# Two layers of attention, short convolution and mixture of experts on one core: router work between the projection's products, counting behind the first gather, constant products in TensorE's pauses, gathered rows taken in halves

## The reference

```python
for i in range(DEPTH):
    xn = rms_norm(h, norm_mix[i])
    mix = sliding_window_attention(...) if i % 2 == 0 else gated_short_conv(...)
    h = h + mix
    h = h + hierarchical_moe(rms_norm(h, norm_ffn[i]), ...)
return rms_norm(h, final_norm)

# inside hierarchical_moe, T tokens
g_prob, g_idx = top_k(softmax(xt @ w_group + b_group), 1)
in_group = (xt @ w_expert + b_expert) of the chosen group
e_prob, e_local = top_k(softmax(in_group), 2)
out[t] = sum over its two experts e of gate * ((silu(x @ g_e) * (x @ u_e)) @ w_down[e])
```

## Time and profile before

| what | us |
|---|---|
| median of three runs | 1453.46 |
| the profiled execution's own time | 1453.89 |
| its span | 1452.2 |
| TensorE busy (matmul) | 1280.6 |
| VectorE / ScalarE / GpSimd busy | 405.7 / 336.3 / 133.2 |
| granted TensorE clock, mean | 0.937 |
| HBM read | 444.96 MB |

### The profile page before, as it was taken

The page is one execution under the profiler, slowest core; times in us unless marked ns, Lnnn a source line. Parts: engine busy times, 40 slices in busy tenths (PEclk is TensorE's granted clock), DMA queues, the critical chain, the costliest instruction groups (busy, mean ns, idle before and its releaser), DMA issues.

```text
span 1452.2 us, 15480 instructions
## 1 busy us (share of the span) xinstructions
PE 1280.6 (88%) x6014; PEld 688.8 (47%) x6014; DVE 405.7 (28%) x867; ACT 336.3 (23%) x632; POOL 133.2 (9%) x109
## 2 busy tenths in 40 slices
PE   5968897998999989999489998799999989999991
PEld 4844675443344333433168877654343433443330
DVE  5376232111111111111455454321111211111114
ACT  3249321221112111221231121212111211121112
POOL 5070020010000000000000000201000100000000
PEclk9978997999999999999779999889999999999996
DMA  9200227999999999999722232479999999999974
GB/s 353 72 1 1 116 115 291 436 429 427 432 432 430 428 429 435 429 429 402 270 60 88 87 118 114 200 318 425 428 434 429 431 428 431 433 429 430 427 298 196
DMA packets 55497, 456.01 MB, mean 314 GB/s; under 512 B 13924, under 2 KB 29310, under 8 KB 38308
## 3 DMA queue, kind: packets, MB, share of 16 engines
q1 hardware_dynamic: 44084, 444.29, 73.0%
q0 software_dynamic: 5120, 8.41, 1.5%
q10 hardware_dynamic: 6256, 2.80, 0.8%
HBM read 444.96 MB, written 18.90 MB: 319 GB/s over the span
## 4 chain that ended last, share of the span: by engine, by line
PE 54%; DMA 35%; DVE 6%; ACT 4%; issue 1%; SPq 0%; POOLq 0%; DVEq 0%; ACTq 0%
DMA big<-in_moe_w_gate_up_dram 33%; PE ps L1015 22%; PE ps L834 19%; PE ps L1033 5%; PE ps L993 3%; DVE xr L1154 1%; PE ps L938 1%; ACT arena L659 1%; ACT arena L675 1%; PE ps L820 1%; PE ps L1005 1%; DVE arena L1249 1%; PE ps L914 1%; DVE h L1293 1%; DVE h L1291 1%
## 5 line engine op out<-in xcount | busy, mean ns | idle before, releaser
L1015 PE MATMUL ps<-big,arena 128*64 128x512 f32 x2048 | 470.5, 615 | 49.8 <-DMA big<-in_moe_w_gate_up_dram 47.3
L1015 PEld LDWEIGHTS ps<-big,arena 128*64 128x64 f32 x2048 | 151.3, 142 | 362.7 <-issue 293.6
L1375 DVE TENSOR_TENSOR gain<-arena,ps 64x512 f32<-64x512 f32 x64 | 68.5, 1070 | 458.8 <-ACT arena L721 458.8
L721 ACT ACTIVATE arena<-ps 64x512 f32<-64x512 f32 x64 | 37.7, 589 | 530.5 <-PE ps L1015 530.5
L540 POOL DMA_INDIRECT rows<-arena x64 | 62.4, 975 | 912.5 <-DVE arena L1401 912.5
L1033 PE MATMUL ps<-small,arena 128*64 128x512 f32 x512 | 116.9, 598 | 0.0
L834 PE MATMUL ps<-xt_parts,small_parts 128*128 128x512 f32 x288 | 112.2, 399 | 1.5 <-DVE xr_parts L1163 1.5
L834 PE MATMUL ps<-xr_parts,small_parts 128*128 128x512 f32 x272 | 107.3, 394 | 0.0
L834 PE MATMUL ps<-xt_parts,big_parts 128*128 128x512 f32 x256 | 100.1, 391 | 0.0
L993 PE MATMUL ps<-arena_parts 128*128 128x512 f32 x256 | 85.5, 416 | 0.0
L993 PE MATMUL ps<-xr_parts,arena_parts 128*128 128x512 f32 x256 | 81.4, 400 | 0.0
(11 more groups left out here) (156 smaller groups left out, 1271.0 us busy)
## 6 DMA issues: line engine op xcount, KB each, us to landing
big<-in_moe_w_gate_up_dram SPq DMA_DIRECT2D x62, 4096.0 KB
small<-in_moe_w_down_dram SPq DMA_DIRECT2D x32, 2048.0 KB, 19.3
arena<-in_moe_w_down_dram SPq DMA_DIRECT2D x16, 2048.0 KB, 18.4
xt<-in_moe_w_down_dram SPq DMA_DIRECT2D x16, 2048.0 KB, 17.8
big<-in_conv_w_in_dram SPq DMA_DIRECT2D x12, 1024.0 KB, 9.2
big<-in_moe_w_gate_up_dram SPq DMA_DIRECT2D x8, 1024.0 KB, 17.6
big<-in_attn_w_qkv_dram SPq DMA_DIRECT2D x1, 4096.0 KB
big<-in_attn_w_o_dram SPq DMA_DIRECT2D x1, 4096.0 KB
```

The costliest lines, as they stand in the source:

```text
L721: nc.scalar.activation(silu[BLOCK:P, j, :], ps[2 + j][0:BLOCK, :], ACT.Silu).then_inc(S.silu_ready, 1)
L1015: mm = nc.tensor.matmul(ps[2 + j][half * BLOCK:(half + 1) * BLOCK, :], xg[:, k, j * BLOCK:(j + 1) * BLOCK], w[:, k, half * FF:(half + 1) * ...
L1375: V.tensor_tensor(hid[BLOCK:P, j, :].rearrange("q (k p) -> q p k", p=P), silu[BLOCK:P, j, :].rearrange("q (p k) -> q p k", p=P), ps[2 + j] ...
```

## The change

Five things: `turn_tile(i, t - 1)` moves into the middle of tile t of the projection, and `logits(t - 1)` behind its second half; ScalarE's and VectorE's copies of tile t-1 move ahead of the norm step of tile t to match; the marks move from `rt` into the tile `silu`, so that counting (`count`) can stand behind the first gather; `keep_busy` multiplies the identity with itself into bank 5, where nobody reads the result, three times before turn(3) and five times after logits(3); and the gathered rows and their transposes are handed over in halves of 512 columns, by three counts of `gathered` and four of `rows_taken` in place of two and two.

```diff
--- before.py
+++ after.py
@@ -179,6 +179,7 @@
         where_f = cut(2)
         where = cut(2).bitcast(I32)
         picked = rt.rearrange("p t c -> p (t c)")
+        marks = silu.rearrange("p a b -> p (a b)")[:, 0:TT * E].rearrange("p (t e) -> p t e", e=E)
         hid = gain[:].rearrange("p (j f) -> p j f", j=2)
 
         early = xt[:].rearrange("p (a k b) c -> p a k (b c)", a=2, k=2)
@@ -623,8 +624,10 @@
 
             def norm(i):
                 for t in range(TT):
+                    if t >= 1 and i in (1, 3):
+                        take_turned(i, t - 1)
                     root(i, t)
-                    if t >= 1 and i < 4:
+                    if t >= 1 and i in (0, 2):
                         take_turned(i, t - 1)
                 if i < 4:
                     take_turned(i, TT - 1)
@@ -702,18 +705,18 @@
 
             def take_picked(S, i):
 
-                act.wait_ge(S.gathered, i * 2 + 1)
+                act.wait_ge(S.gathered, i * 3 + 1)
                 for half in range(2):
-                    ins = nc.scalar.activation(picked[:, half * HALF:(half + 1) * HALF], ps[half][:], ACT.Copy)
-                ins.then_inc(S.rows_taken, 1)
+                    nc.scalar.activation(picked[:, half * HALF:(half + 1) * HALF], ps[half][:], ACT.Copy)\
+                        .then_inc(S.rows_taken, 1)
 
             def take(S, i):
 
-                act.wait_ge(S.gathered, i * 2 + 2)
                 for half in range(2):
-                    ins = nc.scalar.activation(xg[:, 4 * half:4 * half + 4, :],
-                                               ps[half][:].rearrange("p (a b) -> p a b", a=4), ACT.Copy)
-                ins.then_inc(S.rows_taken, 1)
+                    act.wait_ge(S.gathered, i * 3 + half + 2)
+                    nc.scalar.activation(xg[:, 4 * half:4 * half + 4, :],
+                                         ps[half][:].rearrange("p (a b) -> p a b", a=4), ACT.Copy)\
+                        .then_inc(S.rows_taken, 1)
 
             def swish(S, n, j):
 
@@ -939,6 +942,12 @@
                                           start=(d == 0), stop=(d == DT - 1))
                 mm.then_inc(logits_ps, 1)
 
+            def keep_busy(n):
+
+                for _ in range(n):
+                    nc.tensor.matmul(ps[5][:], ident[:], ident[:].unsqueeze(1).to_broadcast([P, 4, P]),
+                                     start=True, stop=True)
+
             def project(first, i, product):
 
                 for t in range(TT):
@@ -952,13 +961,14 @@
                                 mm = product(ps[6 + f % 2][:], t, half, k)
                             if k == DT - 1:
                                 mm.then_inc(mix_ps, 1)
+                            if t >= 1 and half == 0:
+                                turn_tile(i, t - 1)
                     if t >= 1:
-                        turn_tile(i, t - 1)
-                    if t >= 2:
-                        logits(i // 2, t - 2)
-                logits(i // 2, TT - 2)
+                        logits(i // 2, t - 1)
+                keep_busy(3)
                 turn_tile(i, TT - 1)
                 logits(i // 2, TT - 1)
+                keep_busy(5)
 
             def attention_product(bank, t, half, k):
                 if t == 0 and half == 0:
@@ -974,14 +984,16 @@
             def router(l):
                 pe.wait_ge(mask_ready, l + 1)
                 ranks = ps[5][:, 0:TT * E].rearrange("p (t e) -> p t e", e=E)
-                nc.tensor.matmul(ranks[:, 0:TT], upper[:], rt[:, :, 224:256], start=True, stop=False)
+                nc.tensor.matmul(ranks[:, 0:TT], upper[:], marks, start=True, stop=False)
                 for t in range(TT - 1):
                     mm = nc.tensor.matmul(ranks[:, t + 1:TT], ones[:],
-                                          rt[:, t:t + 1, 224:256].to_broadcast([P, TT - 1 - t, E]),
+                                          marks[:, t:t + 1, :].to_broadcast([P, TT - 1 - t, E]),
                                           start=False, stop=(t == TT - 2))
                 mm.then_inc(rank_ps, 1)
+
+            def count(l):
                 for t in range(TT):
-                    mm = nc.tensor.matmul(ps[7][:, 0:E], ones[:], rt[:, t, 224:256], start=(t == 0), stop=(t == TT - 1))
+                    mm = nc.tensor.matmul(ps[7][:, 0:E], ones[:], marks[:, t, :], start=(t == 0), stop=(t == TT - 1))
                 mm.then_inc(rank_ps, 1)
 
             def pick(S, i):
@@ -1000,11 +1012,13 @@
                 for t in range(TT):
                     nc.tensor.matmul(ps[4][:, 0:2], parts(sel[:, t].rearrange("p j s -> p (j s)")), parts(dcol[:, t, :]),
                                      start=(t == 0), stop=(t == TT - 1))
-                pe.wait_ge(S.rows_taken, i * 2 + 1)
                 for d in range(DT):
+                    if d % 4 == 0:
+                        pe.wait_ge(S.rows_taken, i * 4 + d // 4 + 1)
                     mm = nc.tensor.transpose(ps[d // 4][:, (d % 4) * P:(d % 4 + 1) * P],
                                              picked[:, d * P:(d + 1) * P], ident[:])
-                mm.then_inc(S.gathered, 1)
+                    if d % 4 == 3:
+                        mm.then_inc(S.gathered, 1)
 
             def gate_up(S, j, w, cuts=None):
 
@@ -1040,12 +1054,13 @@
                 b0 = BIG_EXPERT[l]
                 pe.wait_ge(x_split, TT * (l + 1))
                 pick(S, 0)
+                count(l)
                 turn_picked(S, 0)
 
                 def up(i, j):
                     big_loaded(pe, b0 + j, i)
                     if j == 0:
-                        pe.wait_ge(S.rows_taken, i * 2 + 2)
+                        pe.wait_ge(S.rows_taken, i * 4 + 4)
                     gate_up(S, j, big[:, big_slot(b0 + j)])
 
                 def turn(m, odd, j):
@@ -1087,7 +1102,7 @@
                                 q = r * PAIRS + i - PAIRS
                                 pick(over[l], q)
                                 turn_picked(over[l], q)
-                                pe.wait_ge(over[l].rows_taken, q * 2 + 2)
+                                pe.wait_ge(over[l].rows_taken, q * 4 + 4)
                                 pe.wait_ge(over[l].where_ready, q + 1)
                                 pe.wait_ge(over_in[l], (r * PAIRS + i + (1 - PAIRS)) * 64)
                                 for j in range(2):
@@ -1278,6 +1293,8 @@
 
                     for half in range(2):
                         f = 2 * t + half
+                        if half == 1 and t >= 1:
+                            take_turned(2 * l + 1, t - 1)
                         dve.wait_ge(mix_ps, 2 * TT * l + f + 1)
                         hs = h[:, t, half * HALF:(half + 1) * HALF]
                         V.tensor_tensor(hs, ps[6 + f % 2][:], hs, ALU.add).then_inc(mix_used, 1)
@@ -1309,7 +1326,7 @@
                 idx = rt[:, :, 120:128].bitcast(U32)
                 gs, s2 = rt[:, :, 128:129], rt[:, :, 129:130]
                 m2 = rt[:, :, 192:224]
-                m12 = rt[:, :, 224:256]
+                m12 = marks
                 io = iota[:, 0:E].unsqueeze(1).to_broadcast([P, TT, E])
                 dve.wait_ge(logits_ps, TT * (l + 1))
                 step(V.tensor_tensor(lg, ps[4][:, 0:TT * NR].rearrange("p (t n) -> p t n", t=TT),
@@ -1379,7 +1396,7 @@
 
             def find_rows(S, i, taken=None):
 
-                dve.wait_ge(S.gathered, i * 2 + 2)
+                dve.wait_ge(S.gathered, i * 3 + 3)
                 if taken is not None:
                     dve.wait_ge(S.row_ready[0], taken)
                 for j in range(2):
```

## The result

The changed kernel takes 1444.86 us (median of five, 1443.28 to 1445.16), the kernel before beside it 1453.46 us: ratio 0.9931, interval 0.9911 to 0.995. On a second chip session it took 1442.0 us against 1454.41, ratio 0.9917, 0.9902 to 0.9932. So it is faster, by 0.7% in one session and 0.8% in the other; 1440.0 was forecast. The profiled execution took 1443.71 us, span 1441.8, 10.4 less than before; 14.6 had been the sum and 13.5 the forecast.

A forecast was written before the change was run, and what follows sets the result against it. Experts bound by weight loads, so each layer's end follows its stream's start, limited by TensorE's path and the DMA backlog. Gains of 7.9 and 6.7 us sum to 14.6, less 1.1 is 13.5: 1440.0 us, range 1438 to 1447.

The forecast's parts named there:

- the sum: First gate/up product of both layers: the lesser gains of the two limits add up to 14.6 us.
- the forecast proper: Whole kernel: 1440.0 us, within 1438 to 1443, given a chance of 0.60.
- rival 1: Clock falls in the router's pause, ranks and gather at half clock in both layers: 6.6 us lost, 1446.6; chance 0.20.
- One of its own signs of being wrong: Gather ahead of the experts: the forecast is wrong if it runs at half clock; 3.85 us was expected.
- The last product pushed by 3.1 and 2.6 us: End of projection: turns and logits between products delay the last one, 3.1 us in layer 0, 2.6 in layer 1.
- The stall of turn(0): Middle of tile 1 of layer 0's projection: the turn waits for its row, 0.5 us.
- Turn(3) at 214.5 us: Behind layer 0's projection: the last turn starts with its row, at 214.5 us for 215.64 before.
- Turn to last logits 3.44 us at full clock: From turn(3)'s start to the end of the last logits: 3.44 us at full clock for 6.24 before.
- Constant products cost nothing as long as the clock is full, and it is full: Waits before turn(3) and under VectorE's router: 0.87 us each, three 2.6 and five 4.4 us, fitting inside the waits.
- Counting and halves: Gather to first gate/up product: 3.2 us for 3.5; counting there eats most of the halves' gain of about 1 us.
- Two limits that tie: Start of the gate/up stream: TensorE's path allows 7.9 and 6.8 us gain, the DMA backlog 7.9 and 6.7.
- The end moves with the start: Experts of each layer: DMA-bound at 428 GB/s, so the layer's end moves with its stream's start, some 7 us earlier.

The follow-up runs named there:

- a4: Changed kernel plus two constant products per layer, one behind turn(3) and one between ranks and first gather: 1442.23 us, ratio 0.9915 to before.
- c4: b4 with one more constant product, between ranks and counting: 1436.95 us, ratio 0.9868 to before.
- a3: Changed kernel with counting back in front of the first gather, marks left in their new place: 1441.64 us, ratio 0.9916 to before.
- c2: Changed kernel with gathered rows handed over whole again, one count for both copies and eight transposes in a row: 1441.58 us, ratio 0.9905 to before.
- b2: a3 with each layer's first gather leaving out the remainder of the tokens (8 of its 16 products): 1440.75 us, ratio 0.9893 to before.
- c1: Kernel before plus only the constant products, three ahead of logits(2) and five behind the last logits: 1441.12 us, ratio 0.9902 to before.
- b1: Changed kernel with turns, logits and copies in the old order, three constants between logits(1) and logits(2): 1440.02 us, ratio 0.9894 to before.
- a1: Changed kernel again without any edit, in the second session: 1442.0 us, ratio 0.9917 to before.
- b4: Changed kernel with old order, earlier VectorE copy of tile 2, counting first, constants ahead of logits(2), behind turn(3) and five under the router: 1437.09 us, ratio 0.9863.
- c3: The same kernel as b4, run again for a second sample: 1437.16 us, ratio 0.9863 to before.
- b3: Changed kernel with ten constant products in place of five under the router: 1446.58 us, ratio 0.9937 to before.

## Why the prediction came out as it did

The sign and the range held, and so did the main mechanism, the clock. The size was too large by 3.1 us in the profiled execution (10.4 for 13.5), by 4.9 on the first medians: 1444.86 lies outside the 1438 to 1443 of the forecast proper and is in the range because this takes in rival 1; the 1442.0 of the second session lies inside. One of its own signs of being wrong came true in part: the gather of layer 1 ran at half clock for 3.4 of its 5.47 us.

- **The last product pushed by 3.1 and 2.6 us:** right, 3.35 and 2.9. The stall of turn(0) was 0.5 us, as worked out.
- **Turn(3) at 214.5 us:** 214.79.
- **Turn to last logits 3.44 us at full clock:** 3.9. A turn that is followed by a wait takes 1.11 us on the chain, not 0.87, and logits behind a copy 1.95, not the 1.71 of those that run on.
- **Constant products cost nothing as long as the clock is full, and it is full:** this step failed. The price of one, 0.87 us, was right. But in each layer the clock fell once, for 3.4 us: in layer 0 the five took 6.06 us and stuck out by 0.8 behind the mask, in layer 1 the gather took 5.47 us, 1.6 too many. I had read the full clock of the 3.7 us from 236.7 as proof that light work with short pauses is safe. The windows of after show 3.5 us of just that, from 214.9, and half clock behind them. Rival 1 had named the router's pause at 6.6 us; what came was about a third of it, 0.8 and 1.6 us. With a constant product in either light stretch (a4, c4) the clock stayed at 1.00, and in c4 it cost nothing; but it also stayed there in some layers without, so how far such a constant can be relied on is open.
- **Counting and halves:** gather to gate/up 3.0 us for 3.2; a3 and c2 give 0.4 against and 0.5 for, as forecast that the one eats the other.
- **Two limits that tie:** partly. With the clock's loss TensorE's path was the later one, by pauses of 1.2 and 2.1 us. The backlog as second limit shows at most in b2, for 0.6 us.
- **The end moves with the start:** right to 0.3 us in both layers.
- **What I had not seen** is that the new order is no part of the gain: I credited the whole path to one change, where c1 and b1 show that constants in the old order do as much. Before, turn(3) came as late as 215.64 us because logits(2) ahead of it ran at half clock; in c1 they run at full clock and turn(3) starts at 213.47, earlier than the row of the changed kernel is there (214.74). Behind the last product the order saves 2.4 us in layer 0 (a1 against b1), and it makes that product 3.4 us late. The sum was right for the kernel as it is; it never asked what the constants would do alone.

Layer by layer, the first gate/up product of layer 0 came 6.4 us earlier for 7.9: product 0.25, turn and logits 0.5, the five 0.8, hops 0.1, less 0.2 behind the gather. Layer 1 gained 4.3 for 6.7: product 0.3, turn and logits 0.5, hops 0.2, gather 1.6, less 0.2.

Why does a3 have a better path than a1 and no better median? For the profiled executions that is shown: from the last gate/up landing of layer 0 to the last scatter it took 45.2 us (661.2 to 706.4) before and in a1, and 46.9 in a3 and b1; in layer 1 it is 45.2 in a1 and 46.9 in a3 again. So a3 loses 3.4 us there, as much as its path had gained. In a3 the clock is at half just then:

```profile
653.80:657.00 3.20, 3.20 (x10) 0.97 (x10) 0.00 (x0) 0.00 (x0) 0.00 (x0) 0.53 1.02 435
```

That stretch is bound by TensorE, and the 14 traces leave no doubt about the price. Of the 27 layer ends in which a gate/up landing stands last on the chain, 14 had no half clock in this stretch and took 45.2 us, 10 had 3.3 to 3.4 us of it and took 46.8 to 46.9, and 3 (a4 and b2 in layer 0, c4 in layer 1) had 6.0 to 6.1 and took 48.1 to 48.2. No edit changes what this stretch takes at full clock (45.2 us before as after), so up to 3 us a layer come and go between traces for nothing that was edited. Whether that also makes the spread of 2 to 8 us between executions of one kernel, and hides what c4 gains over b4, stays open: only one execution of each has a trace.

## What to carry to other kernels

A stretch in which TensorE does little (small products, turns, waits for another engine) in front of dense work pays twice, by its waits and by the clock afterwards; products that compute nothing, put into the waits, took 14 us off this kernel without any other edit. Try one in each light stretch, ahead of the wait, and not all in the longest stretch: the fastest versions here (b4, c3, c4) have one ahead of logits(2) and one behind turn(3). Then read the granted clock of each stretch in the trace, in more than one execution: how many such products there are does not tell it. Before moving work between dense products, ask what hangs on the last of these: here the last tile's whole path through the router did, and 12.6 MB of loads. Work moved ahead of it saved 2.4 us behind it in layer 0 and made it 3.4 us late.

## What the hardware showed that I had not expected

- Half clock behind 3.5 us in which TensorE was busy for 2.63 us with turn, copy wait and logits (0.52 in the window after), where 3.7 us of similar light work elsewhere had left it full; and at 938.7 us behind 3.3 us with 1.08 busy. With one more wide product (0.87 us) in each of the two stretches, a4 and c4 show 1.00 in both layers; a3 shows it without.
- The fall comes at one place in one version and at another in the next (218.5 us in the changed kernel, none in layer 0 of a3 and c2, which are equal up to there), and b4 and c3, the same kernel, differ in layer 0 (half clock in the gather, and none), so a single trace does not say that a stretch is safe.
- Where TensorE is the limit, 3.4 us of half clock cost 1.7 us: 46.9 us for 45.2 in the stretch behind the last landing, 15.65 for 13.95 in the gate/up products of b3.
- A float32 product of 128 columns of weights and 512 columns costs 0.87 us at full clock (4.4 us for five: 4.54 with the tail in c4; 8.66 us for ten in b3), as the reading of the 64-wide pairs had it. By the Trainium skill (TensorEngine Tiling (Array Packing), Tiling Modes), tiles run in parallel; the trace agrees, since two 64-wide products (four of the 64 instructions that take 13.95 us) take the 0.87 us of one wide one.
